# Prompt attention of a hybrid decoder layer: a unit becomes 64 queries of all eight heads instead of 128 queries of four

## What is computed

```python
def mla_attend(q_abs, q_r, q_pos, ckv, kr, k_pos):
    s = (jnp.einsum('bqhr,bkr->bhqk', q_abs, ckv).astype(jnp.float32)
         + jnp.einsum('bqhp,bkp->bhqk', q_r, kr).astype(jnp.float32)) * SOFTMAX_SCALE
    mask = q_pos[:, None] >= k_pos[None, :]
    s = jnp.where(mask[None, None], s, NEG_INF)
    p = jax.nn.softmax(s, axis=-1).astype(ckv.dtype)
    return jnp.einsum('bhqk,bkr->bqhr', p, ckv)
```

## Time and profile before

| | |
|---|---|
| median of three runs | 2125.49 us (2124.41 to 2127.14) |
| the profiled execution | 2128.32 us, of which the span 2126.5 us |
| PE busy over the span | 2085.4 us, 98% |
| PE weight loads | 1953.7 us, 92% |
| DVE, ACT, POOL busy | 1277.5, 972.7, 352.4 us |
| mean granted TensorE clock | 0.994 |
| attention on PE | from 190.6 us to 829.3 us of the span |

### The profile page before, as it was taken

The page is one execution under the profiler, slowest core; times in us unless marked ns, Lnnn a source line. Parts: engine busy times, 40 slices in busy tenths (PEclk is TensorE's granted clock), DMA queues, the critical chain, the costliest instruction groups (busy, mean ns, idle before and its releaser), DMA issues.

```text
span 2126.5 us, 31437 instructions
## 1 busy us (share of the span) xinstructions
PE 2085.4 (98%) x11893; PEld 1953.7 (92%) x11893; DVE 1277.5 (60%) x2689; ACT 972.7 (46%) x1729; POOL 352.4 (17%) x499
## 2 busy tenths in 40 slices
PE   6999999999999999999999999999999999999997
PEld 6998888888888887799999999999999999999997
DVE  7785878778878775465344644456444644446434
ACT  4445766555555555453334423343334433344333
POOL 3443311011100201150004200050002300041000
PEclk9999999999999999999999999999999999999999
DMA  8876321111110204445434453434534453433532
GB/s 303 251 232 184 92 58 38 45 31 31 31 31 16 100 30 155 152 133 168 136 123 128 141 183 113 145 118 144 165 107 153 131 182 116 128 117 120 178 119 73
DMA packets 159557, 260.44 MB, mean 122 GB/s; under 512 B 21323, under 2 KB 109779, under 8 KB 158247
## 3 DMA queue, kind: packets, MB, share of 16 engines
q1 hardware_dynamic: 153470, 237.59, 35.7%
q0 software_dynamic: 2304, 12.58, 1.6%
q10 hardware_dynamic: 3632, 8.28, 1.3%
HBM read 216.97 MB, written 41.66 MB: 122 GB/s over the span
## 4 chain that ended last, share of the span: by engine, by line
PE 56%; DVE 1%; DMA 0%; ACT 0%; issue 0%; ACTq 0%; POOLq 0%; POOL 0%; DVEq 0%
PE b_ps L122 56%; PE b_ps L2100 1%; DMA d_ws<-in_w 0%; DVE d_y L1988 0%; ACT d_wr L1241 0%; DVE d_y L2008 0%; DVE d_wr L84 0%; DVE d_y L1990 0%; ACT d_y L1889 0%; POOLq L1619 0%; ACT d_zs L1882 0%; ACTq L1619 0%; ACT d_zs L1865 0%; DVE d_gate_p L2016 0%; DVE d_pool L84 0%
## 5 line engine op out<-in xcount | busy, mean ns | idle before, releaser
L122 PE MATMUL b_ps<-d_ht,d_wr 128*128 128x412 f32 x3840 | 734.8, 349 | 1.0 <-DVE d_wr L84 0.7
L122 PEld LDWEIGHTS b_ps<-d_ht,d_wr 128*128 128x128 f32 x3840 | 715.8, 188 | 5.1 <-issue 1.8
L84 DVE TENSOR_TENSOR d_wr<-d_ws,d_wr 128x1024 fp32r<-128x1024 f32 x260 | 321.3, 1236 | 550.7 <-ACT d_wr L1241 550.7
L1241 ACT ACTIVATE d_wr<-d_ws 128x1024 fp32r<-128x1024 f32 x260 | 275.1, 1058 | 600.6 <-PE b_ps L122 591.7
L746 PE MATMUL b_ps<-kt,k_qs 128*128 128x512 f32 (+2 forms) x1520 | 337.3, 370 | 1.6 <-DVE b_p L1090 1.5
L746 PEld LDWEIGHTS b_ps<-kt,k_qs 128*128 128x128 f32 x1520 | 265.7, 188 | 47.5 <-DVE b_p L1090 2.4
L84 DVE TENSOR_TENSOR b_pt<-b_ps,b_pt 128x512 fp32r<-128x512 f32 x272 | 183.5, 689 | 95.4 <-ACT b_pt L1044 93.5
L1044 ACT ACTIVATE b_pt<-b_ps 128x512 fp32r<-128x512 f32 x272 | 158.7, 597 | 174.0 <-PE b_ps L1150 115.3
L1150 PE MATMUL b_ps<-b_pt,kv 128*128 128x512 f32 x816 | 229.6, 410 | 3.6 <-DVE b_pt L84 3.6
L1037 ACT ACTIVATE b_p<-b_p,b_bias 128x1024 f32<-128x1024 f32 (+7 forms) x192 | 171.5, 896 | 54.4 <-DVE b_low L1097 53.4
L122 PE MATMUL b_ps<-d_mrg,d_wr 128*128 128x412 f32 x960 | 189.8, 353 | 0.0
(11 more groups left out here) (212 smaller groups left out, 2066.0 us busy)
## 6 DMA issues: line engine op xcount, KB each, us to landing
d_ws<-in_w SPq DMA_DIRECT2D x260, 512.0 KB, 3.6
out_q<-a_qout SPq DMA_DIRECT2D x32, 384.0 KB, 4.7
d_hf<-out_ht SPq DMA_DIRECT2D x20, 412.0 KB, 3.5
d_olf<-out_olat SPq DMA_DIRECT2D x40, 206.0 KB, 2.9
a_xt<-in_x_t SPq DMA_DIRECT2D x16, 512.0 KB, 5.2
out_ht<-a_hf SPq DMA_DIRECT2D x16, 512.0 KB, 3.7
out_olat<-b_ol SPq DMA_DIRECT2D x32, 256.0 KB, 4.2
out_y<-d_y SPq DMA_DIRECT2D x5, 1536.0 KB
```

The source lines that it names most:

```text
L84: return e.tensor_tensor(low, source, high.bitcast(f32), ALU.subtract)
L122: mm = pe.matmul(out, stationary(a, k), moving(b, k), start=first and k == 0 and a + b == 0, stop=last and k == depth - 1 and a == 1)
L1241: act.activation(ahead["wr"][k % 2][:, 0, :, :], ahead["ws"][k % 4][:, :, :], ACT.Copy).then_inc(ahead["w_hi"], 1)
```

## The change

A unit becomes 64 queries (`BLK`) of all eight heads. The score partitions of a stationary block are now 64 queries of two heads, so a unit still has four blocks of 128, and there are still 32 units. Unit u takes the query block `query_block(u)`: the two units that shared a tile now take its first and its second half. The first half's unit sees 64 keys fewer. Where its number of keys is no multiple of 128 the last key tile has 64 rows (`tile_rows`): its four transposes have 64 stationary columns and write 64 partitions, H and L handle 64 partitions, and V contracts 64 rows.

`key_chunks` cuts a unit's keys into the same number of chunks as before but as equal as multiples of 64 allow. For chunks that begin and end at multiples of 64, `kt` is laid out as [part, 2048 keys], and the new tokens' keys get a buffer `kt_new`. The mask covers the last 64 keys. `takes` and `loaded` get the new sizes and other landing times.

In DRAM `q` keeps its layout, so `load_q` now reads pieces of 64 queries for eight heads, 256 bytes each, where it read 2 KB (latent part) and 512 bytes (rotary part). The store of a unit's result writes pieces of 256 bytes instead of 512. In `project` the loads of units 4 and 5 move from step NT+2 to `LAST_STEP`, behind the last two stores of queries.

```diff
-                if i in (NT + 1, NT + 2):
+                if i in (NT + 1, LAST_STEP):
 
                     sp.wait_ge(lat_ok, NT)
-                    for u in (2 * (i - NT), 2 * (i - NT) + 1):
+                    for u in (2, 3) if i < LAST_STEP else (4, 5):
                         load_q(sp, io, keep, u)
...
-def query_tile(u):
-
-    return FIRST_TILES[u // NGRP] if u < SMALL else u // NGRP
+def query_block(u):
+
+    return u % 2 + 2 * (FIRST_TILES[u // 2] if u < SMALL else u // 2)
+
+
+def key_count(u):
+
+    return BLK * (query_block(u) + 1)
+
+
+def key_tiles(u):
+
+    return -(-key_count(u) // P)
+
+
+def tile_rows(u, j):
+
+    return min(P, key_count(u) - j * P)
...
-    sp.dma_start(qf[:, 0, :, :], io["q"][i, :, g, 0:HG, :]).then_inc(q_in, 16)
+    by_group = lambda a: a.rearrange("p (g h) t -> p g h t", g=NGRP)
+    sp.dma_start(by_group(qf[:, 0, :, :]), io["q"][i, :, :, 0:HG, at:at + BLK]).then_inc(q_in, 16)
     for half in range(2):
-        turned = io["q"][i, :, g, HG + half, :].rearrange("(h f) t -> f h t", h=HG)
+        turned = io["q"][i, :, :, HG + half, at:at + BLK].rearrange("(h f) g t -> f g h t", h=HG)
...
-    qs, out = keep["qs"][high_slot(u)], keep["ps"][n % NS][:, 0:size * P]
+    qs, out = keep["qs"][high_slot(u)], keep["ps"][n % NS][:, 0:size]
...
-        mm = pe.matmul(out, qs[:, a, h, :], keep["kt"][:, first:first + size, b, :],
+        mm = pe.matmul(out, qs[:, a, h, :], keep["kt"][:, b, first:first + size],
                        start=k == 0, stop=k == len(pairs) - 1)
...
-def key_chunks(tiles):
-
-    sizes = [4] * (tiles // 4) + [tiles % 4] * (tiles % 4 > 0)
-    if tiles > 4 and tiles % 4 == 1:
-        sizes[-2:] = [3, 2]
-    return [(sum(sizes[:c]), size) for c, size in enumerate(sizes)]
+def key_chunks(u):
+
+    blocks = key_count(u) // BLK
+    count = -(-blocks * BLK // 512)
+    ends = [blocks * c // count * BLK for c in range(count + 1)]
+    return [(ends[c], ends[c + 1] - ends[c]) for c in range(count)]
...
-            return 5 * max(0.111, 0.0586 * key_chunks(tiles(u))[step[3]][1])
+            return 5 * max(0.111, 0.0586 / P * key_chunks(u)[step[3]][1])
...
-                sp.dma_start(io["olat"][:, HG * g:HG * g + HG, i * P:i * P + P],
-                             ol[u % 2][:, :].rearrange("p (h t) -> p h t", h=HG)).then_inc(o_out[u % 2], 16)
+                sp.dma_start(io["olat"][:, :, at:at + BLK],
+                             ol[u % 2][:, :].rearrange("p (h t) -> p h t", h=NH)).then_inc(o_out[u % 2], 16)
...
-                        mm = pe.transpose(ps_t[n % NTB][:, h * P:h * P + P],
-                                          weights(u, h, slice(j * P, j * P + P)), ident[:, :])
+                        mm = pe.transpose(ps_t[n % NTB][0:tile_rows(u, j), h * P:h * P + P],
+                                          weights(u, h, slice(j * P, j * P + tile_rows(u, j))), ident[:, :])
...
-                        mm = pe.matmul(ps_o[u % 2][:, :], kv[:, j, a, :], pt[n % NPT][:, b, :],
+                        mm = pe.matmul(ps_o[u % 2][:, :], kv[0:tile_rows(u, j), j, a, :], pt[n % NPT][0:tile_rows(u, j), b, :],
```

More of the change, by code:

```diff
@@ L63 @@
 RUN = PAST // P
+BLK = P // 2
 QUAD = 4
@@ L1030, in _ @@
                     at = row(u, h)
-                    span = weights(u, h, slice(part * PART * P, min(tiles(u), (part + 1) * PART) * P))
+                    span = weights(u, h, slice(part * PART * P, min(key_count(u), (part + 1) * PART * P)))
                     negated = chunks(u) == 1
@@ L1127, in _ @@
                     n = number[step]
-                    first, keys = key_chunks(tiles(u))[c]
+                    first, keys = key_chunks(u)[c]
                     if h == 0 and c == 0:
```

73 lines of the change are left out of this document (40 added, 33 removed).

## The result

The changed kernel is slower: 2136.64 us (median of 7 runs, 2133.55 to 2137.62) against 2125.49 for the kernel before (7 runs, 2124.01 to 2130.15), a ratio of 1.0051 with a 95% interval of 1.0042 to 1.0060. The forecast was 2111 us, in a range from 2107 to 2118. The span of the profiled execution went from 2126.5 to 2135.8 us. Two slow executions of the last kernel in the table of experiments (2971 and 4168 us, of six) are left out of its median, and no other run is.

A forecast was written before the change was run, and what follows sets the result against it. The prediction took PE's instruction stream to bound attention; 9.1 (score columns) + 3.2 (store ahead) + 2.4 (clock) = 14.7 us off the median of 2125.5 gave 2110.8, rounded 2111 us, in a range from 2107 to 2118.

The forecast's parts named there:

- What bounds the kernel: Attention: PE is busy all the time from 300 on, so what leaves its instruction stream leaves the span.
- only two places are odd: Stretches of attention: only 200 to 210 (PE idle, clock 0.71 and 0.61) and 736 to 738 (a shorter hole) stand out.
- Score columns: PE's score matmuls in attention: fewer columns, priced by runs of equal matmuls, save 9.1 us.
- Transposes and value products: PE on half key tiles: 64 narrow transposes and 48 value matmuls of 64 rows cost the same as full ones, nothing saved.
- The store that goes ahead: Start of attention near 200: the last staged queries' store, issued before units 4 and 5's loads, saves 3.2 us before first V.
- What is late next is unit 4: After the first V: unit 4's loads, issued some 1 us later, must land by about 202; the tightest place.
- The clock: Behind the idle stretch at 200: full clock for the nine V and 25 small scores saves 2.4 us.
- Smaller packets: DMA queues in attention: 256-byte packets take 3.2 us a unit on 16 engines, hidden by the unit's length; no cost.
- The starved loads by small packets: Rival, first eight units: loads of 256-byte packets come too late and PE waits, ending at 2131 us; chance 0.04.
- Only the columns: Rival: the store lands late or the clock falls anyway, saving 9.1 and at most 1 more, 2116 us; chance 0.20.
- Half-wide transposes: Rival, half key tiles: transposes of 64 columns cost half, 3.5 us more saved, 2107.5 us; chance 0.05.
- Many small waits: Rival, throughout attention: the new order of steps makes PE wait some 8 us in all, 2119 us; chance 0.07.

The follow-up runs named there:

- last kernel in the table of experiments: Kernel with interleaved stores, but loads of queries and stores of results in the 2 KB and 512-byte pieces of the kernel before: 2114.1 us, ratio 0.9951.
- columns given back: Kernel with interleaved stores, but the first score chunk of every unit with half a tile is 64 unread columns wider: 2124.19 us, ratio 1.0001.
- pieces of before: Changed kernel, but all loads of queries and stores of attention results move in pieces of 2 KB and 512 bytes: 2124.29 us, ratio 0.9997.
- V on 128 rows: Changed kernel, but copies H and L and value products of all 16 half tiles take 128 rows, transposes stay narrow: 2131.20 us, ratio 1.0027.
- the stores first: Changed kernel, but SyncE issues unit 0's store before the pages' and decode queries' loads, unit 1's before the loads of units 8 and 9: 2128.96 us.
- full rows: Changed kernel, but the last key tile of the 12 half-tile units from unit 8 on is zero-filled and worked at 128 rows: 2132.53 us, ratio 1.0029.
- interleaved stores: Changed kernel with full rows, SyncE's stores of results put between loads from unit 6 on, decode's loads behind unit 6's store: 2118.43 us, ratio 0.9965.
- the pieces of before in the stores: Changed kernel, but only the stores of attention results go in 512-byte pieces, loads of queries stay at 256 bytes: 2130.80 us, ratio 1.0026.

## Why the prediction was wrong

**What bounds the kernel.** Right for the body of attention: PE at 100.00 of 100 us after as before. The reading "only two places are odd" was the flaw of method: it looked for places that had stalls, not for waits that were just in time.

**Score columns (a saving of 9.1 us).** Priced right: 448 columns cost 0.200 us where the forecast had 0.204, the score matmuls take 9.8 us less in one pair of profiles and the columns given back 8.0 more in the other. Given back they moved the time by 5.8 us only; 1.6 us less idle time of PE is a part of the difference.

**Transposes and value products (nothing).** This step failed. The transposes are nothing, as forecast. The value products were priced by their 512 moved columns alone; the change of the row count from 128 to 64 and back, an operation that no row of before showed, should have been bounded from both sides and was not. It costs 0.34 us a half tile, 5.4 us in the experiment with 128 rows in all 16 and 4.1 us in the one with full rows in 12.

**The store that goes ahead (3.2 us).** The step is right by itself: it is worth 5.1 us in the kernel before, where the first V then doesn't wait. Of these 5.1 up to 1.5 us may be the idle time at 737, which that profile doesn't have either. In the changed kernel PE still waited 1.61 us at the first V, and ACT's first H 2.10 for the store's landing, both more than the bound of 1 us. The first V at 199.87 (199 to 200 forecast) is luck in part, for attention began 1.35 us sooner in this execution (189.25 against 190.60). The cause is the small pieces again: the loads of units 2 and 3, ahead of the four stores, hold SyncE until 191.11, and until 189.07 with the pieces of before, where this wait is gone. The prediction took the issue time of these loads from the kernel before. "What is late next is unit 4" was the wrong answer to the right question. Late next was ACT's O of unit 2. The prediction listed the queue that the moved stores pass, and not who waits on the transfers further back in that queue, nor whether the new order of steps makes anyone come sooner. ACT was ready 7.9 us sooner, with a reserve of 4.0.

**The clock (2.4 us).** At 200 it stayed at 1.00 in the profile after, but not because of the half microsecond of idle time that the prediction argued with: the wait was 1.61. Behind waits of about this length the nine V took 2.56 us in the profile after and 2.36 with V on 128 rows (a wait of 1.60), but 3.79, 3.77 and 4.07 with the stores first, full rows and interleaved stores (1.69, 1.73 and 1.74), and 4.02 behind 1.50 with the pieces of before in the stores. So the term came true in this profile by luck. It was lost again behind the new hole, where the clock stood at 0.50 for ten microseconds.

**Smaller packets (nothing on the path).** This step failed too, and it turned the sign: with the pieces of before everywhere the same program takes 12.3 us less. The prediction priced the packets by the time of the DMA engines (16.7 ns each) and found room for them. That price was near, 3.8 us a unit against 3.2, but two costs that are on the path were left out. SyncE's issue grew from 0.43 to about 0.61 us a transfer, and it is serial: 20 transfers of units 6 to 9 and more stand before the first store. And the store's landing grew from 4.2 to 6.6 us for ten alike. The number of pieces doubled as their size was halved, and no run parts the two. The sum had both load and store "hidden" by the length of a unit, but a store's landing is not hidden by the unit's length where a buffer is awaited.
The Trainium skill ("DMA: Bandwidth & Descriptors", Specifications) puts 512 bytes as the least transfer for line rate. The prediction took the row's two thirds per packet as the answer to it; by the landing of whole stores the trace agrees with the skill in direction, with 6.6 us in pieces of 256 bytes against 4.2 in pieces of 512.

**Sum of the miss.** From after to the interleaved kernel with large pieces are 22.5 us. Taken in one order they are 12.3 for the pieces, 4.1 for the rows, and the remaining 6.1, by difference, for the order on SyncE. The split depends on that order, for the costs overlap in the same waits: with the order on SyncE mended and full rows the pieces are worth only 4.3. The forecast was 14.7 us below the kernel before, and this last kernel is 10.4 below it. The last four half tiles are 1.4 of what is missing; the rest is open.

**Rivals.** The starved loads by small packets (0.04) had the right cause and the right sign, and the wrong place: not the loads' landing by bandwidth, but the issue time and a store's landing. The test it set, 43 ns a packet, would have called it off. "Only the columns" named one thing that came true, the store that lands late behind the larger loads of units 2 and 3, and its 2116 us were missed all the same. "Half-wide transposes" fell. "Many small waits" is there with 1.1 us in three waits of PE between 582 and 643, not with 8. Faster got 0.92: the chances were spread over sizes of gain, and none over a wait that the profile shows only as its absence.

## What to carry to other kernels

Where a change makes one engine come sooner or a queue go slower, list every wait on a DMA in the next tens of microseconds that had no idle time before, and its reserve: issue, landing, and when the waiting instruction was reached. Where the order of steps is found by a program, compare the new order with the old one, and name the unit of each row before reading a reserve from it. Price smaller pieces at the issuing engine and at the landing that a buffer waits for, not only at the DMA engines' share; and put the stores that free a buffer ahead of loads that nobody needs yet. A dimension that is cut in half for a few instructions only (here the rows of a value product) is to be bounded as an operation the trace does not show: here filling it up with zeros was cheaper.

## What the runs showed of the hardware

- A group of three matmuls of 64 rows between groups of 128 rows loses 0.34 us, with PE's weight loads idle for 0.17 us ahead of it and 0.37 behind. Two kernels without the change of rows (and with the copies at 128 rows too) don't have it. Why the loads wait there is open.
- A weight load of 64 stationary columns took 111 ns against 140 for 128 in the transposes, and four such transposes 0.60 us as four full ones.
- SyncE's issue of a load of 256-byte pieces took 0.61 to 0.63 us, of 512-byte ones 0.43. Stores of 256 KB landed in 6.6 us in 1024 pieces, in 4.2 in 512.
- Behind 12.48 us of idle PE the granted clock was 0.50 from 225 to 235. A wait of 1.61 us left it at 1.00 in one execution; in three others the mean of 195 to 210 was 0.89, 0.75 and 0.70 around waits of 1.74, 1.73 and 1.69 us.
- The idle time of 1.54 us at 737 that the prediction left in place is not in the profile after.
